# Transposed activations 64 bytes further up, and what lies behind them 128, in a hybrid attention and recurrence layer in split fp32

## What is computed

```python
proj = x @ w_in[l]                                   # 2048 -> 2048+256+256+2560+2560+4096
q, k, v, rx, ry, gl = jnp.split(proj, SPLIT_POINTS, axis=-1)
y_attn = sliding_window_attention(q, k, v, sinks) @ w_attn_proj[l]
rx = causal_dwconv(rx, rnn_conv_w[l], rnn_conv_b[l])
hr = rg_lru(rx, lru_wa[l], lru_ba[l], lru_wi[l], lru_bi[l], lru_lambda[l])
y_rnn = (hr * jax.nn.gelu(ry, approximate=True)) @ w_rnn_proj[l]
g_attn, g_rnn = jnp.split(jax.nn.sigmoid(gl + b_gate[l]), 2, axis=-1)
mix = (g_attn * y_attn + g_rnn * y_rnn) @ w_out[l]
x = layer_norm(ALPHA * x + mix, ln1_g[l], ln1_b[l])
up = x @ ffn_w_up[l]
gate = causal_dwconv(x @ ffn_w_gate[l], ffn_conv_w[l], ffn_conv_b[l])
f = (jax.nn.gelu(gate, approximate=True) * up) @ ffn_w_down[l]     # d_ff 6144
x = layer_norm(ALPHA * x + f, ln2_g[l], ln2_b[l])
```

## The kernel before

| tiles | offset from BASE before | mod 128 | after | mod 128 |
|---|---|---|---|---|
| `raw` | 0 | 0 | 0 | 0 |
| `w_hi` (slots of 5120) | 40960 | 0 | 40960 | 0 |
| `w_lo` (slots of 5120) | 61440 | 0 | 61440 | 0 |
| `act_t` | 81920 | 0 | 81984 | 64 |
| `const`, `par`, `stats` and other small ones: `SMALL` | 114688 | 0 | 114752 | 64 |
| `g_t`, `o_t`, `res`, `x_tok`, all at `BIG` | 118336 | 64 | 118464 | 64 |
| `f_t` (`BIG` + 32768), `s_buf`, `xc_hi`, `xc_lo`, `lru_w_hi`, `lru_w_lo`: `BIG` + a multiple of 512 | | 64 | | 64 |

## Time and profile before

### The profile page before, as it was taken

One profiled execution on the slowest core, in us unless ns is written; L12 is line 12 of the kernel. 1 busy time (PEld: TensorE's weight loads), 2 busy tenths in 40 slices (PEclk: granted clock), 3 DMA queues, 4 the chain that ended last, 5 costly groups with the idle time before them and its releaser, 6 DMA issues.

```text
span 1785.5 us, 32091 instructions
## 1 busy us (share of the span) xinstructions
PE 1746.6 (98%) x13020; PEld 1663.1 (93%) x13020; DVE 1033.6 (58%) x1182; ACT 845.2 (47%) x1027; POOL 50.9 (3%) x34
## 2 busy tenths in 40 slices
PE   7999999999999999999988999999999999999996
PEld 7999999999999999999878999998889999999885
DVE  5695695444455656555668555555444555555455
ACT  5567566444346666544444444444333434343332
POOL 0000000000000000000003000000000000000002
PEclk9999999999999999999998999999999999999998
DMA  8464453565544343455744555565555555555551
GB/s 292 138 207 157 143 198 130 183 210 191 187 146 152 131 165 124 160 189 189 282 141 142 188 181 176 184 227 194 188 185 183 178 187 188 178 176 187 188 189 70
DMA packets 157141, 317.14 MB, mean 178 GB/s; under 512 B 6008, under 2 KB 11800, under 8 KB 156312
## 3 DMA queue, kind: packets, MB, share of 16 engines
q1 hardware_dynamic: 157080, 316.28, 53.4%
HBM read 314.16 MB, written 2.10 MB: 177 GB/s over the span
## 4 chain that ended last, share of the span: by engine, by line
PE 95%; DVE 3%; ACT 1%; DMA 0%; issue 0%; SPq 0%; ACTq 0%; DVEq 0%
PE bank L268 70%; PE bank L295 19%; PE bank L491 2%; DVE w_lo L246 1%; PE bank L561 1%; PE bank L548 1%; PE bank L280 1%; DVE act_t L1162 1%; PE bank L539 0%; DMA x_tok<-in_x_dram 0%; DVE res L1223 0%; DVE res L1219 0%; PE bank L463 0%; PE bank L563 0%; ACT w_hi L239 0%
## 5 line engine op out<-in xcount | busy, mean ns | idle before, releaser
L268 PE MATMUL bank<-act_t,w_hi 128*128 128x256 f32 x5952 | 1084.4, 285 | 15.8 <-DVE act_t L1162 10.9
L246 DVE TENSOR_TENSOR w_lo<-raw,w_hi 128x1024 fp32r<-128x1024 f32 (+1 forms) x552 | 703.4, 1286 | 648.6 <-ACT w_hi L239 648.5
L239 ACT ACTIVATE w_hi<-raw 128x1024 fp32r<-128x1024 f32 (+1 forms) x552 | 601.0, 1095 | 792.7 <-PE bank L268 584.4
L268 PEld LDWEIGHTS bank<-act_t,w_hi 128*128 128x128 f32 x5952 | 933.1, 193 | 20.6 <-issue 17.0
L268 PE MATMUL bank<-act_t,w_lo 128*128 128x256 f32 x2976 | 845.1, 284 | 0.0
L268 PEld LDWEIGHTS bank<-act_t,w_lo 128*128 128x128 f32 x2976 | 574.3, 193 | 0.0
L295 PE MATMUL bank<-w_hi,f_t 128*128 128x512 f32 x768 | 241.9, 396 | 0.0
L295 PEld LDWEIGHTS bank<-w_hi,f_t 128*128 128x128 f32 x768 | 144.4, 188 | 34.7
L295 PE MATMUL bank<-w_lo,f_t 128*128 128x512 f32 x384 | 151.9, 396 | 0.0
L268 PE MATMUL bank<-g_t,w_hi 128*128 128x256 f32 x640 | 113.1, 280 | 0.0
L268 PEld LDWEIGHTS bank<-g_t,w_hi 128*128 128x128 f32 x640 | 97.7, 187 | 0.0
(11 more groups left out here) (137 smaller groups left out, 960.1 us busy)
## 6 DMA issues: line engine op xcount, KB each, us to landing
raw<-in_w_in_dram SPq DMA_DIRECT2D x52, 1024.0 KB, 5.0
raw<-in_ffn_w_gate_dram SPq DMA_DIRECT2D x48, 1024.0 KB, 5.2
raw<-in_ffn_w_up_dram SPq DMA_DIRECT2D x48, 1024.0 KB, 5.2
raw<-in_ffn_w_down_dram SPq DMA_DIRECT2D x48, 1024.0 KB, 5.1
raw<-in_w_in_dram SPq DMA_DIRECT2D x32, 1280.0 KB, 5.9
raw<-in_w_rnn_proj_dram SPq DMA_DIRECT2D x16, 1280.0 KB, 6.1
raw<-in_w_attn_proj_dram SPq DMA_DIRECT2D x16, 1024.0 KB, 5.2
raw<-in_w_out_dram SPq DMA_DIRECT2D x16, 1024.0 KB, 5.1
```

Source lines behind the costliest of these rows:

```text
L239: nc.scalar.activation(w_hi[:, slot, 0:size], raw[:, chunk, half:half + size], ACT.Copy)\
L246: nc.vector.tensor_tensor(w_lo[:, slot, 0:size], raw[:, chunk, half:half + size], w_hi[:, slot, 0:size].bitcast(F32), ALU.subtract).then_i ...
L268: last = nc.tensor.matmul(dst, w[:, slot, at_ % size:at_ % size + P], moving[:, kt, part, :], start=(kt == 0 and n == 0 and c % 2 == 0), s ...
```

## The change

`act_t` is placed 64 bytes further up, the small tables behind it go with it, and everything from `BIG` on is placed 128 bytes further up. `raw`, `w_hi`, `w_lo` and what lies inside them (`raw_tail`, `gate_sig`, `q_now`) stay. On each engine the instructions and their order are the same.

```diff
-        act_t = at("act_t", 81920, [P, KT, 2, T], F32R)
-        SMALL = 81920 + 32768
+        act_t = at("act_t", 81920 + 64, [P, KT, 2, T], F32R)
+        SMALL = 81920 + 64 + 32768
...
-        BIG = SMALL + 3648
+        BIG = SMALL + 3648 + 64
```

## The result

The changed kernel takes 1758.14 us (median of 4 runs, 1753.6 to 1759.1) against 1786.51 us (4 runs, 1784.3 to 1787.09): a ratio of 0.9838, 95% interval 0.9823 to 0.9853, so 1.6% faster. The prediction said 0.8% faster and a range down to 1764. The profiled execution spans 1756.6 us, 28.9 less than the one of before.

The account below looks back on a forecast made before the run. TensorE's matmul pace, set by the operands' byte distance modulo 128, was taken as the bound. Terms -18.1 + 2.5 + 0.6 = -15.0 us turned the median of 1785.95 us into 1771.0, 0.8% faster; range 1764 to 1781 us.

Parts of the forecast that it names:

- What bounds the kernel: Whole kernel: TensorE, busy 98% of the span, sets the time through its pace from one matmul's start to the next.
- Term 1: act_t moving in panel_features: distance 0 becomes 64, 2.1 ns less on each of 8616 matmuls, 18.1 us gained.
- Term 2: act_t stationary in panel_tokens, the output projection: 384 matmuls slow from 226.8 to 233.4 ns, 2.5 us lost.
- Term 3: The 96 matmuls of line 280 (value columns), w moving, act_t stationary: 6.6 ns more each, 0.6 us lost.
- Term 4: The 164 transposes, const moving: distance goes from 64 to 0, taken as 0, at most 2.2 us.
- term 6: VectorE and ScalarE: offsets of this kind don't show in their times, so 0.
- Term 5: g_t and o_t moving, f_t stationary: distance 64 to 192, the same modulo 128, so 0.
- the rival that said so: Distance counts modulo 256 with sign: g_t and o_t lose 15.4 us, f_t gains 10.3, time 1776; chance 11%.
- the recorded sign of a period of 256: In the changed kernel's chain, g_t and o_t above 120 ns and f_t below 226 would show period 256.
- offsets do nothing: Offsets of 64 bytes have no effect on the matmul paces: time 1786, or 1789 with losses; chance 13%.
- the cover gives out: TensorE waits for VectorE's split in the recurrence, whose 1920 matmuls gain nothing: 4.0 us, time 1775; chance 5%.
- slower: Only the loss counts, 6.6 ns where the moving stream lies 64 behind: +6.9 us, time 1793; chance 8%.

Follow-up runs that it names:

- (64, 64, 64): w_hi, w_lo, act_t, the small tables and BIG all 64 bytes up against the kernel before, raw left in place: 1786.34 us, ratio 1.0001.
- BIG alone: Only BIG and what lies at it 128 bytes up against the kernel before, act_t and small tables unmoved: 1773.55 us, ratio 0.993.

## Why the prediction was wrong

- **What bounds the kernel**: right. The time went with the paces of TensorE's stream, read from the chain; in the changed kernel VectorE, ScalarE and the DMAs cost it a microsecond at most (its waits grew by 0.2 us for w_lo and 0.2 for s_buf, and the attention's stage gained 1.2 us less than the paces say).
- **Term 1**, act_t moving: 18.1 us forecast, 19.0 measured; the second FFN half came to 271.36 us, forecast 271.5. **Term 2**, act_t stationary: 2.5 forecast, 2.5 measured. That a distance seen in one tile carries over to another, at the same width, is shown by these two, and (64, 64, 64) shows that the address itself doesn't count.
- **Term 3**, line 280: 0.6 us of loss forecast from f_t's row; its records became 4 ns shorter instead (283 to 279), so a gain of some 0.4 us. The row at 512 columns was the wrong neighbour for 256.
- **Term 4** and **term 6**, transposes and the other engines: nothing, as forecast.
- **Term 5**, g_t, o_t and f_t: this is the step that failed. It took the distance modulo 128, found 64 before and after, and priced 1728 + 1152 matmuls at 0. They gained 7.6 + 5.2 = 12.8 us, which is nearly all of the 13.4 between forecast and result, and without act_t's shift they gain 12.8 (BIG alone). The period is 256; no row of the kernel before could tell 128 from 256, and the rival that said so was there with 11%.
- **Luck in the size**: the later runs show a second pace at just these distances, 117.8 at D 192 and 233.3 at D 64, and these are the paces that g_t, o_t and f_t had before. On them the tiles would have gained nothing, and the time would have been about 1758.1 + 12.8 = 1770.9 us (an estimate from these pieces), the forecast 1771.0 with the same step wrong. In the profiled executions of the change and of BIG alone all of these stages took the faster pace; how often they do is not known.
- **That rival's price** was wrong in sign. It gave g_t and o_t 126.6 ns, by adding the 6.6 ns that f_t's use had cost at the same distance; they took 113.3. The effect at 256 columns doesn't follow from the one at 512, and a price carried from the one to the other should have had both signs in its bounds. With 8.9 ns either way on 1728 matmuls, 15 us, the range would have reached down to 1749. For the same reason the recorded sign of a period of 256, g_t and o_t above 120, was one-sided: the period is 256, and they fell.
- The rivals *offsets do nothing*, *the cover gives out* and *slower* are out: act_t's 64 bytes are worth 15 us (1773.55 with BIG alone, 1758.14 with both), TensorE's waits are nearly as before, and g_t and o_t gained.

## What to carry to other kernels

When TensorE bounds a kernel that loads weights for every matmul, divide long pieces of its chain by their counts, one for each pair of tiles, and compare the paces; if they differ with the same widths, look at the byte distance of the two tiles modulo 256, and try the eight multiples of 32. Measure each such distance in the role and width in which it will be used, profile more than one execution, and take the spread of the times as part of the result: some distances have two paces, and a faster TensorE can begin to wait where it did not. Where an unseen effect is bounded by a row of another width, bound it with both signs.

## What the hardware showed that I had not expected

The pace of a stream of matmuls, each with its own weight load, hangs on the byte distance modulo 256 of the streaming tile and the one being loaded: 113.3 to about 120 ns for 256 columns, 226.7 to 234.3 for 512, at the granted clock of 1.00. The Trainium skill ("TensorE: Matmul & The Clock Gate", Part 2, step 1) has the two reads independent; the trace disagrees, by up to 6.7 ns a matmul. Where between the tiles and the array the two meet, no run here shows.

At D 0, 64 and 192 the steady values are in steps. Over three matmuls, the high-high, low-high and high-low of one product, the time beyond one cycle a column is 16 cycles of 2.4 GHz times a whole number: 3 x 113.3 ns is 816 cycles, 768 + 3 x 16; 117.8 is 768 + 5 x 16, 120.0 is 768 + 6 x 16; at 512 columns 226.7, 228.9 and 233.3 are 1536 + 6, 7 and 9 x 16. The other distances don't fit: 116.7 at D 32 is 768 + 4.5 x 16, 118.7 at D 128 is 768 + 5.4 x 16. 16 elements are 64 bytes. That a collision costs one line of 64 bytes is my reading of these numbers, not shown by a run.

And one program has more than one speed: at D 192 with 256 columns and at D 64 with 512, a stage of up to 2304 matmuls runs at one of two paces for its whole length, and another execution of the same program can take the other, so that the four times of one kernel lay between 1732.64 and 1754.83 us. D 128 and D 160 with 256 columns have two paces as well, seen within one execution each. What sets the pace is open.
